# Narrower level products in a blockwise triangular inverse, inside a streaming encoder layer

## The reference

```
out = concat([o_attn, o_rw]) @ w_out
# attention group, per block of 64 queries:
p = softmax(mask(q_lat @ ckv.T + q_rope @ krope.T)); o = p @ ckv
# recurrent group (RWKV-7), per head, state S is 64 x 64:
for t in tokens:
    sa = S @ (-kk_t)
    S  = S * w_t + outer(sa, kk_t * a_t) + outer(v_t, k_t)
    y_t = S @ r_t
```

## Time and profile before

| | |
|---|---|
| median of 3 runs | 2221.33 us (2218.11 to 2222.33) |
| profiled execution, its own time | 2222.09 us |
| its span, first to last instruction | 2220.3 us |
| TensorE busy | 1904.7 us, 86% |
| TensorE weight loads busy | 1674.3 us, 75% |
| VectorE / ScalarE / GpSimd busy | 1007.9 / 630.4 / 206.6 us |
| stage with the recurrence and the attention | about 458 us to 1125 us of the span |

### The profile page before, as it was taken

The page is one execution under the profiler, slowest core; times in us unless marked ns, Lnnn a source line. Parts: engine busy times, 40 slices in busy tenths (PEclk is TensorE's granted clock), DMA queues, the critical chain, the costliest instruction groups (busy, mean ns, idle before and its releaser), DMA issues. The chain is left out here.

```text
span 2220.3 us, 40096 instructions
## 1 busy us (share of the span) xinstructions
PE 1904.7 (86%) x16490; PEld 1674.3 (75%) x16490; DVE 1007.9 (45%) x1567; ACT 630.4 (28%) x1209; POOL 206.6 (9%) x285
## 2 busy tenths in 40 slices
PE   4999974279899899998951985999999999999996
PEld 3999952146767666676731974999999999999995
DVE  4676354644454454454537029242334233423347
ACT  4423343023434434434422225212111211121114
POOL 0000000022432232322400000100000000000000
PEclk8999998579999999999985998999999999999998
DMA  8453116521010100100041203111101101110122
GB/s 300 133 159 124 47 40 173 157 89 44 19 35 30 35 20 31 35 19 21 10 145 51 86 19 109 39 57 48 34 34 58 48 20 48 58 48 20 48 110 81
DMA packets 108759, 148.89 MB, mean 67 GB/s; under 512 B 66384, under 2 KB 81360, under 8 KB 108144
## 3 DMA queue, kind: packets, MB, share of 16 engines
q1 hardware_dynamic: 108592, 146.46, 20.4%
HBM read 115.95 MB, written 30.50 MB: 66 GB/s over the span
## 5 line engine op out<-in xcount | busy, mean ns | idle before, releaser
L397 PE MATMUL ps<-hhi,whi 128*128 128x364 f32 (+1 forms) x1728 | 573.5, 332 | 81.9 <-DVE wlo L390 48.0
L397 PE MATMUL ps<-hlo,whi 128*128 128x364 f32 (+1 forms) x1728 | 572.7, 331 | 0.0
L397 PE MATMUL ps<-hhi,wlo 128*128 128x364 f32 (+1 forms) x1728 | 572.3, 331 | 0.0
L397 PEld LDWEIGHTS ps<-hhi,whi 128*128 128x128 f32 x1728 | 329.0, 190 | 84.0 <-issue 68.4
L397 PEld LDWEIGHTS ps<-hlo,whi 128*128 128x128 f32 x1728 | 329.1, 190 | 0.0
L397 PEld LDWEIGHTS ps<-hhi,wlo 128*128 128x128 f32 x1728 | 328.8, 190 | 0.0
L390 DVE TENSOR_TENSOR wlo<-wraw,whi 128x1024 fp32r<-128x1024 f32 x74 | 90.5, 1224 | 407.5 <-ACT whi L386 405.5
L743 POOL TENSOR_TENSOR nlev<-gm,con 64x256 f32<-64x256 f32 x204 | 156.1, 765 | 245.4 <-DVE gm L1364 231.3
L1601 DVE TENSOR_TENSOR acc<-acc,ps 128x364 f32<-128x364 f32 (+1 forms) x240 | 126.6, 531 | 101.8 <-PE ps L2009 101.8
L2009 PE MATMUL ps<-ahi,dhi 128*128 128x364 f32 (+1 forms) x480 | 158.5, 330 | 2.4 <-DVE acc L1601 2.4
L2009 PE MATMUL ps<-alo,dhi 128*128 128x364 f32 (+1 forms) x480 | 157.5, 328 | 0.0
(11 more groups left out here) (216 smaller groups left out, 2579.0 us busy)
## 6 DMA issues: line engine op xcount, KB each, us to landing
wraw<-in_w_tiles SPq DMA_DIRECT2D x72, 512.0 KB, 3.4
late<-in_ada_t SPq DMA_DIRECT2D x32, 512.0 KB, 3.3
ci<-scan SPq DMA_DIRECT2D x17, 768.0 KB, 4.5
draw<-in_w_down SPq DMA_DIRECT2D x20, 512.0 KB, 3.3
slab<-in_ada_w SPq DMA_DIRECT2D x4, 2048.0 KB, 19.0
scan<-mix SPq DMA_DIRECT2D x12, 512.0 KB, 4.3
x<-in_x_t SPq DMA_DIRECT2D x4, 1456.0 KB, 10.7
x<-x_mid SPq DMA_DIRECT2D x1, 4352.0 KB, 13.2
```

Of the source, the lines that this page charges most:

```text
L397: mm = nc.tensor.matmul(ps[:, 3 * u + c, 0:n], w[u][:, k, :], x[:, k, a:a + n], start=(k == 0 and w is whi and x is hhi), stop=(k == KD - ...
```

## The change

Joining blocks of size m changes, in the upper triangular inverse, only the columns whose index has bit l set, and in its transpose only the columns whose index has it clear: 32 of 64. The change moves only these through the level's products:

- `level_x`: the moving operand is the 32 columns of the transpose with bit l clear, in runs of m (`half_columns(..., l, 0)`); its result, 32 columns a head, lies packed in PSUM.
- `level_copy`: 128 x 128 elements from packed PSUM to the half columns of `xt[l]`. Each level has its own tile now, whose other columns stay zero, because the tile also serves as 64-column weights.
- `level_t`: both products move 32 columns a head, and both results lie packed in one half bank each.
- `invert_level`: one addition of 128 x 256 elements (packed PSUM, half columns of `tt`); 128 x 128 in the last level.
- `tt` has the transpose first and then the inverse, so that one access pattern reaches the half columns of both.
- GpSimd zeroes the five `xt` tiles once, between `prepare(0, 0)` and the first slot. Four of them lie where `krope` was, so it first waits for the outputs stored from there and for the copies of `krope`. ScalarE waits for the zeroes before the first copy.

Weights, their loads, the number of matmuls and all DMAs stay.

```diff
+        xt2, xt3, xt4, xt5, end = place(WA - 2 * T * 4, *((f"xt{l}", [P, PAIRS, C]) for l in range(2, LEVELS)))
+        def half_columns(ap2, l, side):
+            return ap2.rearrange("p (b h m) -> p b h m", h=2, m=2 ** l)[:, :, side, :]
+        def half_bank(r, l, at):
+            return ps[r, WB, at:at + C // 2].rearrange("p (b m) -> p b m", m=2 ** l)
...
             prepare(0, 0)
+            pool.wait_ge(stored, 16 * 3)
+            pool.wait_ge(krope_copied, 2)
+            pool.wait_ge(c_k, 2 + 1)
+            for l in range(1, LEVELS):
+                nc.gpsimd.memset(xt[l][:, :, :], 0.0).then_inc(xt_zero, 1)
+            pool.wait_ge(xt_zero, LEVELS - 1)
             slot_pool(0, 0)
...
-                nc.scalar.copy(xt[:, :, :].rearrange("p a b -> p (a b)"), ps[:, WB, 0:PAIRS * C]).then_inc(c_xev, 1)
+                nc.scalar.copy(half_columns(xt[l][:, :, :].rearrange("p a b -> p (a b)"), l, 0),
+                               ps[:, WB, 0:PAIRS * C // 2].rearrange("p (b m) -> p b m", m=2 ** l)).then_inc(c_xev, 1)
...
-                t2 = tt[u][:, 0:n, :, :].rearrange("p a b c -> p (a b c)")
-                nc.vector.tensor_tensor(t2, t2, ps[:, WB, 0:n * PAIRS * C], ALU.add).then_inc(c_tev, 1)
+                if l < LEVELS - 1:
+                    both = tt[u][:, 0:2 * (2 * half + m)].rearrange("p (e x) -> p e x", e=2)[:, :, 0:2 * half]
+                    both = both.rearrange("p e (q h m) -> p e q h m", h=2, m=m)[:, :, :, 0, :]
+                    new = ps[:, WB, 0:2 * half].rearrange("p (e q m) -> p e q m", e=2, m=m)
+                else:
+                    both = half_columns(tt[u][:, 2 * half:4 * half], l, 1)
+                    new = ps[:, WB, half:2 * half].rearrange("p (q m) -> p q m", m=m)
+                nc.vector.tensor_tensor(both, both, new, ALU.add).then_inc(c_tev, 1)
...
-                    x = tt[u][r, 1, p, :] if l else con[r, K_EYE2:K_EYE2 + C]
-                    mm = nc.tensor.matmul(ps[r, WB, C * p:C * p + C], nlev[r, l, p, :], x, start=True, stop=True)
+                    if l:
+                        mm = nc.tensor.matmul(half_bank(r, l, C * p // 2), nlev[r, l, p, :], half_columns(lower(u)[r, p, :], l, 0), start=True, stop=True)
+                    else:
+                        mm = nc.tensor.matmul(ps[r, WB, C * p:C * p + C], nlev[r, l, p, :], con[r, K_EYE2:K_EYE2 + C], start=True, stop=True)
...
-                    mm = nc.tensor.matmul(ps[r, WB, C * p:C * p + C], xt[r, p, :], tt[u][r, 0, p, :], start=True, stop=True)
+                    mm = nc.tensor.matmul(half_bank(r, l, C * (PAIRS + p) // 2), xt[l][r, p, :], half_columns(upper(u)[r, p, :], l, 1), start=True, stop=True)
                 if l < LEVELS - 1:
                     for p, e, r in per_head():
-                        mm = nc.tensor.matmul(ps[r, WB, C * (PAIRS + p):C * (PAIRS + p) + C], tt[u][r, 0, p, :], xt[r, p, :], start=True, stop=True)
+                        mm = nc.tensor.matmul(half_bank(r, l, C * p // 2), upper(u)[r, p, :], half_columns(xt[l][r, p, :], l, 0), start=True, stop=True)
```

More of the change, by code:

```diff
@@ L50 @@
 LEVELS = 6
+TT = 2 * PAIRS * C + C
 SF = 6
@@ L231, in build @@
         assert end <= R1
-        cum, pinc0, pneg, bk, ar0, vv, gm0, tt0, xt, bktm0, uv, st0, st1, rhs, end = place(
+        cum, pinc0, pneg, bk, ar0, vv, gm0, tt0, xt1, bktm0, uv, st0, st1, rhs, end = place(
             WA, ("cum", [P, PAIRS, C + 1]), ("pinc0", [P, PAIRS, C + 1]), ("pneg", [P, PAIRS, C]), ("bk", [P, PAIRS, 2 * C]),
             ("ar0", [P, PAIRS, 2 * C]), ("vv", [P, PAIRS, 2, C]), ("gm0", [P, 2, PAIRS, 2 * C]),
-            ("tt0", [P, 2, PAIRS, C]),
-            ("xt", [P, PAIRS, C]), ("bktm0", [P, PAIRS, P]), ("uv", [P, PAIRS, P]), ("st0", [P, PAIRS, DH]), ("st1", [P, PAIRS, DH]),
+            ("tt0", [P, TT]),
+            ("xt1", [P, PAIRS, C]), ("bktm0", [P, PAIRS, P]), ("uv", [P, PAIRS, P]), ("st0", [P, PAIRS, DH]), ("st1", [P, PAIRS, DH]),
             ("rhs", [P, PAIRS, C]))
@@ L241, in build @@
         assert end <= R1
+        xt2, xt3, xt4, xt5, end = place(WA - 2 * T * 4, *((f"xt{l}", [P, PAIRS, C]) for l in range(2, LEVELS)))
+        assert end <= WA - T * 4
+        xt = [None, xt1, xt2, xt3, xt4, xt5]
         gm1, end = place(WA - T * 4, ("gm1", [P, 2, PAIRS, 2 * C]))
         assert end <= WA
-        nlev, tt1, end = place(RAW_AT, ("nlev", [P, LEVELS, PAIRS, C]), ("tt1", [P, 2, PAIRS, C]))
+        nlev, tt1, end = place(RAW_AT, ("nlev", [P, LEVELS, PAIRS, C]), ("tt1", [P, TT]))
         assert end <= MIX_AT
@@ L317, in build @@
         kk_raw, kk_sq, kk_mm, kk_root, pre_done = sem("kk_raw"), sem("kk_sq"), sem("kk_mm"), sem("kk_root"), sem("pre_done")
-        state_in, state_ready = sem("state_in"), sem("state_ready")
+        state_in, state_ready, xt_zero = sem("state_in"), sem("state_ready"), sem("xt_zero")
         scan_out, bg_out = sem("scan_out"), sem("bg_out")
@@ L495, in slot_units, with lower, upper @@
             return sum(SLOT_UNITS if x < SLOTS - 1 else LAST_SLOT_UNITS for x in numbers)
+        def lower(u):
+            return tt[u][:, 0:PAIRS * C].rearrange("p (a b) -> p a b", a=PAIRS)
+        def upper(u):
+            return tt[u][:, PAIRS * C:2 * PAIRS * C].rearrange("p (a b) -> p a b", a=PAIRS)
+        def half_columns(ap2, l, side):
+            return ap2.rearrange("p (b h m) -> p b h m", h=2, m=2 ** l)[:, :, side, :]
+        def half_bank(r, l, at):
+            return ps[r, WB, at:at + C // 2].rearrange("p (b m) -> p b m", m=2 ** l)
         def over_tiles(ap2, k):
@@ L951, in level_copy @@
                 act.wait_ge(c_tmm, (LEVELS - 1) * j + l)
-                nc.scalar.copy(xt[:, :, :].rearrange("p a b -> p (a b)"), ps[:, WB, 0:PAIRS * C]).then_inc(c_xev, 1)
+                if isinstance(j, int) and j == 0 and l == 1:
+                    act.wait_ge(xt_zero, LEVELS - 1)
+                nc.scalar.copy(half_columns(xt[l][:, :, :].rearrange("p a b -> p (a b)"), l, 0),
+                               ps[:, WB, 0:PAIRS * C // 2].rearrange("p (b m) -> p b m", m=2 ** l)).then_inc(c_xev, 1)
             def right_side(i):
@@ L1371, in invert_first @@
                 at_least(dve, c_umm, j)
-                step.mark(nc.vector.tensor_tensor(tt[u][:, 0, :, :], nlev[:, 0, :, :], eye4, ALU.add))
+                step.mark(nc.vector.tensor_tensor(upper(u), nlev[:, 0, :, :], eye4, ALU.add))
                 dve.wait_ge(c_xmm, LEVELS * j + 1 + 1)
-                nc.vector.tensor_tensor(tt[u][:, 1, :, :], ps[:, WB, 0:PAIRS * C].rearrange("p (a b) -> p a b", a=PAIRS), eye4, ALU.add).then_inc(c_tev, 1)
+                nc.vector.tensor_tensor(lower(u), ps[:, WB, 0:PAIRS * C].rearrange("p (a b) -> p a b", a=PAIRS), eye4, ALU.add).then_inc(c_tev, 1)
                 step.wait()
             def invert_level(j, u, l):
-                n = 2 if l < LEVELS - 1 else 1
+                half, m = PAIRS * C // 2, 2 ** l
                 dve.wait_ge(c_tev, LEVELS * j + l)
                 dve.wait_ge(c_tmm, (LEVELS - 1) * j + l + 1)
-                t2 = tt[u][:, 0:n, :, :].rearrange("p a b c -> p (a b c)")
-                nc.vector.tensor_tensor(t2, t2, ps[:, WB, 0:n * PAIRS * C], ALU.add).then_inc(c_tev, 1)
+                if l < LEVELS - 1:
[6 more added lines that the diff above has]
+                nc.vector.tensor_tensor(both, both, new, ALU.add).then_inc(c_tev, 1)
             def next_state(i, u, last):
@@ L1811, in solve @@
                 for p, e, r in per_head():
-                    mm = nc.tensor.matmul(ps[r, WB + 1, C * p:C * p + C], tt[u][r, 0, p, :], rhs[r, p, :], start=True, stop=True)
+                    mm = nc.tensor.matmul(ps[r, WB + 1, C * p:C * p + C], upper(u)[r, p, :], rhs[r, p, :], start=True, stop=True)
                 mm.then_inc(c_umm, 1)
```

## The result

The changed kernel took 2239.25 us (median of 6 runs, 2230.24 to 2243.19); the kernel before, run beside it, 2219.70 us (6 runs, 2214.83 to 2222.33). The ratio is 1.0083, interval 1.0061 to 1.0105: slower by 0.8%, where 2214 us was forecast. The profiled execution took 2243.19 us, its span 2241.4 us.

The account below looks back on a forecast made before the run. The prediction took TensorE's queue to bound the recurrence stage. Pace 0, next shape 3.0 and shorter additions and copies 4.4 made 7.4 us off the 2221.33 us median, say 2214, with a range of 2206 to 2225.

Parts of the forecast that it names:

- the step that held the clock: TensorE in the recurrence stage: unchanged loads and product count, and line 1903's 64-column products, would keep the clock up.
- the rival of the falling clock: Recurrence stage: less streaming drops the clock, 30 us of work at 1.2 GHz, 2244 us in all; chance 13%.
- Pace of the level products: TensorE's level products: weight loads, not streams, set the pace, so halving the streams saves 0 there.
- The first rival: TensorE's level products: the stream sets the pace, some 50 us more come off, 2164 us; chance 5%.
- Next shape 27 ns sooner: TensorE after level groups: the next shape's load starts 0.027 us sooner at 129 gaps, 3.5 us, taken as 3.0.
- The second rival: TensorE: a fixed product cost covers 32 and 64 columns alike, only 4.4 us come off, 2217 us; chance 14%.
- Shorter additions and copies: VectorE's level additions and ScalarE's copies: halved elements shorten TensorE's waits by 4.4 us.
- the third rival: VectorE and ScalarE: short runs cost as the whole, only TensorE's 3.0 us come off, 2218 us; chance 8%.
- Zeroed tiles: GpSimd before its first slot: zeroing five tiles, 1.6 us, fits in its idle time and adds 0.
- Sum: Whole kernel: 0 + 3.0 + 4.4 = 7.4 us off, giving 2214 us.

Follow-up runs that it names:

- kernel with wide streams: Against the changed kernel, all level products stream 64 columns again, while ScalarE and VectorE still handle only half columns: 2217.02 us, ratio 0.9984 to the kernel before.

## Why the prediction was wrong

What failed is the step that held the clock: **"the weight loads and the number of products stay, and line 1903's products with 64 columns kept the clock up"**, which left the rival of the falling clock at 13%. The loads and records did stay (9027 matmuls in the stage for 9025), and the clock fell from 0.98 to 0.93. The weight loads don't keep it up: with 8 columns they are all there and it is 0.79. And products of 64 columns are no witness for products of 32, since where the load sets the pace, every column taken away leaves the array idle for as long. The forecast had worked out this pace, had written that half of the array's time would be free in 108 us of products, and then took it for the lesser argument. That rival came true, and its size was near: it had 30 us of work at the lower level, thus 60 us there, against 68.4 us added, and 30 us of cost for 28. From the whole it took 7.4 and came to 2244; measured 2239.25 and 2250.20. The near size is luck: the twentieth of the stage's work that it assumed rests on no row. Its price, 0.5 for each microsecond at 1.2 GHz, was too high: a level group takes 0.81 us there and not twice 0.46. The range ended at 2225 and left this case out.

The Trainium skill, TensorE: Matmul & The Clock Gate, section LDWEIGHTS, was used for the price of a load. By its rule a load takes 53 ns for 64 columns and 27 for 32. The traces agree to within some 5 ns: a pair of records took 58 ns (461 a group) whatever was streamed, and 31 ns (246 a group) with 32 columns of weights.

The steps of the sum, at equal clock:

- **Pace of the level products, 0:** right. 461 ns a group with 64, 32 and 8 columns. The first rival, that the stream sets the pace, would have needed groups of about 0.25 us.
- **Next shape 27 ns sooner, 3.0 us in all:** right. 203 ns became 176. The trace of before has 140 such gaps and not the 129 that were counted, so that 3.8 us and not 3.5 is the bound. The stage with all streams narrow is 2.1 to 3.7 us shorter at equal clock than with wide ones (633.7, 635.3 for 637.4). The second rival, a fixed cost from which nothing comes off, falls: 64 to 32 columns took off 27 ns, and 32 to 8 another 20, in both steps 0.83 ns a column. The rule of the Trainium skill, TensorEngine Tiling (Array Packing), section Instruction Overhead, that few columns take as long as 60, isn't borne out by these gaps.
- **Shorter additions and copies, 4.4 us:** right for the waits that were counted, low in all. Line 1417 took 421 and 286 ns, the copy 266, as forecast; the third rival, short runs at 687 ns, falls. The kernel with wide streams shows this term by itself. Its waits of TensorE in 475 to 1130 us, line 1941 being line 1903 of before:

```profile
PE ps L1941 <- issue: 12.9, 14, 1.8
PE ps L1941 <- DVE oatt L1501: 11.8, 12, 1.6
...
PE ps L1819 <- ACT vz L1017: 3.8, 6, 1.0
```

  That is 24.7 us where it was 27.8, 3.1 less for 3.2 forecast; the waits of the level products on the copy and the addition are 1.1 less for 1.2. But TensorE's whole idle time in the stage went from 54.4 us (657.00 less 602.56 busy) to 48.4 (655.60 less 607.21), 6.1 less, and the stage is 6.9 us shorter than before at equal clock. Some 2 us of the rest are waits of line 1781 that the forecast had not counted. On ScalarE's `vz` the products of level 0, line 1819 here, wait for 3.8 us, before it was

```profile
PE ps L1781 <- ACT vz L989: 4.9, 7, 1.0
```

  and its short waits of "issue" went from 1.2 us to 0.2.
- **Zeroed tiles, 0:** right. They stand at 467.3 to 468.4, and GpSimd idled 3.35 us behind them until its first slot.
- **Sum:** 7.4 forecast, 9 to 10.6 measured at equal clock (644.3 less 635.3 and 633.7). All of it, and 17.5 us more, went to the clock.

Shown by experiment: that the narrow streams of the level products are the cause (wide streams alone bring clock and time back), and that runs are not, nor a changed order of waits. Argued, not shown: that their density counts and not their width. Open: why 1360 narrow records in `level_x` cost nothing and as many in `level_t` do; `level_x` stands between other work, and the two products of `level_t` follow each other without a break, but no run moved them apart. Open as well: what lets the clock fall in the first place, since the same wait has a fall in one kernel and none in the other, and why the wide-stream kernel has 13.7 us more at 1.2 GHz than before with the same streams. It may be chance or may come of the changed order of busy and idle time; a second profile of before would show how much is chance.

The best version is the one with `level_x` alone narrow and the shorter additions: 2215.13 and 2217.04 us beside 2219.49 and 2218.07, ratios 0.9983 and 0.9984, ahead of both kernels. The one with wide streams has 0.9984 too; the two can't be told apart.

## What to carry to other kernels

Where weight loads set the pace of small products, narrower streams save nearly nothing and can cost the clock: reckon with the time that the array will no longer stream, and look whether the stage already has stretches at the lower clock. Take the saving on the engines that read the result, by reading half of a wide result, and leave the stream as wide as the load. Compare kernels chunk by chunk where both have the same clock, then count the time at 1.2 GHz; a mean time alone would have hidden a gain of some 10 us and a loss of some 28.

## What was not expected of the hardware

- Less streaming made a kernel slower by 4%: with 8 for 64 columns in 3808 of some 9000 records of the stage, at an unchanged full-clock pace of 461 ns for 16 records, the mean clock fell from 0.98 to 0.79.
- The loss varies from run to run: 2237.24 to 2252.52 us in four runs of the changed kernel on one chip (before, 2214.30 to 2223.96 in 24), and 99.4 or 139.9 us at 1.2 GHz in two profiles.
- A group of 16 records with weights of 32 columns and 32 moved took 246 ns, little more than half of the 461 ns with 64 and 64.
- After a fall the clock can stay at 1.2 GHz although TensorE's records leave almost no gap: 17.1 us with 0.04 us idle, where with wide streams it was back after 6.8 us.
- VectorE's additions through runs of 2 to 16 elements took as long as contiguous ones (421 ns for 256, before 420), whether the result in PSUM was packed or its half columns were picked out.
